# Two mixer stages in another order: attention worked between the heads' projections, the recurrence between the convolved columns and the output gates

## The reference

```
proj = h @ w_in          # columns: q 512, k 512, v 512 | qk 512, v 512, o 512, gates 8
# differential attention: 4 heads x 2 halves of 64, rotary q and k, mask by chunks of 64
a = softmax(q1 k1) - lam * softmax(q2 k2);  y_da = rmsnorm(a v) * (1 - lam_init)
# recurrence: 4 heads of 64 x 128
qk = silu(causal_conv(qk));  w = exp(D - m) * (q k);  y_ml = sigmoid(o) * rmsnorm((w v) / den)
y = concat(y_da, y_ml) @ w_out
```

## Time and profile before

| | |
|---|---|
| runs of the kernel | 2193.6, 2198.66, 2198.86 us (median 2198.66) |
| the profiled execution: time, span | 2192.0 us, 2190.2 us |
| PE, PEld, DVE, ACT, POOL busy | 91%, 66%, 38%, 29%, 2% of the span |
| mixer 0, from its gates to the next stage's first turned rows | 1331.90 to 1453.02 us |
| mixer 1, the same | 1864.90 to 1987.13 us |
| mean granted clock of the PE | 0.97 |

### The profile page before, as it was taken

One profiled execution on the slowest core, in us unless ns is written; L12 is line 12 of the kernel. 1 busy time (PEld: TensorE's weight loads), 2 busy tenths in 40 slices (PEclk: granted clock), 3 DMA queues, 4 the chain that ended last, 5 costly groups with the idle time before them and its releaser, 6 DMA issues.

```text
span 2190.2 us, 38271 instructions
## 1 busy us (share of the span) xinstructions
PE 1989.8 (91%) x17232; PEld 1452.0 (66%) x17232; DVE 827.9 (38%) x1259; ACT 627.5 (29%) x994; POOL 46.3 (2%) x99
## 2 busy tenths in 40 slices
PE   5998898888979898888979999789999999979998
PEld 3544344446764444444469988679988987957996
DVE  4111111115530111111165546655545555755552
ACT  2000000004520000000055445554435444555441
POOL 0000000000000000000000000010000000000000
PEclk8999999999999999999999999999999999989999
DMA  9899999995559999999955554236545554424552
GB/s 383 365 426 427 426 427 426 426 427 211 181 197 427 426 426 427 426 427 427 417 199 195 182 184 154 78 107 217 177 158 207 194 184 157 151 79 162 175 191 77
DMA packets 56768, 599.74 MB, mean 274 GB/s; under 512 B 6544, under 2 KB 6800, under 8 KB 9488
## 3 DMA queue, kind: packets, MB, share of 16 engines
q1 hardware_dynamic: 55440, 593.75, 68.4%
q10 hardware_dynamic: 1152, 3.41, 0.6%
HBM read 596.08 MB, written 1.05 MB: 273 GB/s over the span
## 4 chain that ended last, share of the span: by engine, by line
PE 66%; DMA 18%; DVE 6%; ACT 6%; issue 3%; POOL 1%; SPq 0%; DVEq 0%; POOLq 0%; ACTq 0%
PE PS L515 13%; PE PS L517 13%; PE PS L516 13%; PE PS L667 12%; DMA RING<-in_w_down 8%; PE PS L637 7%; DMA WK<-in_w_down 6%; DMA WK<-in_w_up 3%; PE PS L614 2%; PE PS L695 2%; ACT SPLIT L1300 1%; ACT JK L1294 1%; DMA RING<-in_units 1%; DVE SPLIT L1769 1%; POOL SM L474 1%
## 5 line engine op out<-in xcount | busy, mean ns | idle before, releaser
L1769 DVE TENSOR_TENSOR SPLIT<-RING,SPLIT 128x2048 fp32r<-128x2048 f32 (+2 forms) x178 | 400.9, 2258 | 265.7 <-ACT SPLIT L1300 265.5
L667 PE MATMUL PS<-RING,WK 128*32 128x512 f32 x816 | 367.8, 605 | 51.1 <-DMA RING<-in_w_down 29.4
L515 PE MATMUL PS<-HTH,SPLIT 128*128 128x256 f32 x1344 | 382.6, 285 | 0.0
L516 PE MATMUL PS<-HTL,SPLIT 128*128 128x256 f32 x1344 | 380.7, 283 | 0.0
L517 PE MATMUL PS<-HTH,SPLIT 128*128 128x256 f32 x1344 | 380.6, 283 | 0.0
L1300 ACT ACTIVATE SPLIT<-RING 128x2048 fp32r<-128x2048 f32 (+2 forms) x178 | 334.2, 1885 | 142.4 <-DMA RING<-in_units 132.3
L667 PEld LDWEIGHTS PS<-RING,WK 128*32 128x32 f32 x816 | 86.9, 111 | 294.5 <-issue 261.5
L515 PEld LDWEIGHTS PS<-HTH,SPLIT 128*128 128x128 f32 x1344 | 258.1, 192 | 0.5
L516 PEld LDWEIGHTS PS<-HTL,SPLIT 128*128 128x128 f32 x1344 | 258.1, 192 | 0.2
L517 PEld LDWEIGHTS PS<-HTH,SPLIT 128*128 128x128 f32 x1344 | 258.1, 192 | 0.0
L637 PE MATMUL PS<-RING,WK 128*32 128x128 f32 x7104 | 231.6, 274 | 10.6 <-issue 7.5
(11 more groups left out here) (331 smaller groups left out, 2019.7 us busy)
## 6 DMA issues: line engine op xcount, KB each, us to landing
RING<-in_units SPq DMA_DIRECT2D x171, 1024.0 KB, 4.9
RING<-in_w_gate SPq DMA_DIRECT2D x56, 2048.0 KB, 25.6
RING<-in_w_up SPq DMA_DIRECT2D x55, 2048.0 KB, 26.5
RING<-in_w_down SPq DMA_DIRECT2D x53, 2048.0 KB, 29.4
WK<-in_w_down SPq DMA_DIRECT2D x9, 2048.0 KB, 30.0
WK<-in_w_up SPq DMA_DIRECT2D x9, 2048.0 KB, 27.4
WK<-in_w_gate SPq DMA_DIRECT2D x8, 2048.0 KB, 24.8
RING<-in_w_down SPq DMA_DIRECT2D x3, 1024.0 KB, 21.7
```

What stands on the lines that cost most here:

```text
L515: pe.matmul(out, ll, rh, start=start, stop=False)
L516: pe.matmul(out, lh, rl, start=False, stop=False)
L667: t = pe.matmul(PS[32 * i:32 * i + 32, 4 + h, :], mo.HE[:, pb, 32 * f:32 * f + 32], v[:, c, 512 * h:512 * h + 512], start=f == 0, stop=f == 3)
L1769: dv.tensor_tensor(unit_part(u, 1), loaded(u), unit_part(u, 0).bitcast(F32), ALU.subtract).then_inc(s_lo, 1)
```

## The change

The lists of the mixer are rewritten; the number of matmuls, conversions and transfers stays. A head's q and k now lie side by side in one unit (u0+4 to u0+7), and the columns come after them (u0+8, u0+9). The heads use two PSUM banks instead of four, since banks 6 and 7 now serve the attention, so `head(i)` waits for the end of `rotate(i-2)` on DVE. The scores, probabilities and outputs of an attention head follow its projections; then come the columns; the output gates (`gate_rows`, once `last_rows`) stand between the steps of the recurrence, and the attention's results are turned there too. The recurrence's result is turned one row block at a time between the `out` steps, and all of block 1's `out` steps stand at the end. The exponentials of the recurrence move to a buffer of their own. POOL takes two short roots for the attention instead of a long one.

Of the lists of steps only the lines of after stand here (a "+" marks a line that was not there in the place before); the three lists are those of the PE, ACT and DVE, in this order. Line numbers of after are higher: `lo` is 1792, `hi` 1314, the DVE's part of `rotate` 2240 to 2245, of `scores` 2253 and 2257.

```diff
-HEAD_BANK = [5, 6, 7, 4]
-HEADS = [("q", 0), ("q", 1), ("k", 0), ("k", 1), ("q", 2), ("q", 3), ("k", 2), ("k", 3)]
-KEY_AT = [2, 3, 6, 7]
+HEAD_BANK = [5, 4]
...
-            def column(h):
-                u = u0 + 4 + h // 2
...
             def head(i):
-                u = u0 + 6 + i // 2
+                u = u0 + 4 + i // 2
                 hi, lo = unit_pair(u)
                 o = 128 * (i % 2)
                 pe.wait_ge(s_lo, u + 1)
-                pe.wait_ge(*((s_qkc, 4 * l + i + 1) if i < 4 else (s_qr, 4 + 8 * l + i - 3)))
+                if i == 1:
+                    pe.wait_ge(s_gv, 6 * l + 3)
+                elif i >= 2:
+                    pe.wait_ge(s_qr, 4 + 8 * l + i - 1)
                 for c in range(8):
-                    t = three(pe, pair(PS[:, HEAD_BANK[i % 4], 0:256]), (hi[:, c, o:o + 128], lo[:, c, o:o + 128]), both(c),
+                    t = three(pe, pair(PS[:, HEAD_BANK[i % 2], 0:256]), (hi[:, c, o:o + 128], lo[:, c, o:o + 128]), both(c),
                               c == 0, c == 7)
...
             def rotate(i):
                 pe.wait_ge(s_tq, 4 + 8 * l + i + 1)
-                pe.matmul(PS[:, HEAD_BANK[i % 4], 256:512], cs("swap"), mx.TQ[:, i % 2, :], start=True,
+                pe.matmul(PS[:, HEAD_BANK[i % 2], 256:512], cs("swap"), mx.TQ[:, i % 2, :], start=True,
                           stop=True).then_inc(s_sw, 1)
...
+            def column(i):
+                u = u0 + 8 + i // 2
...
+                if i == 0:
+                    pe.wait_ge(s_unc, 2 * l + 2)
+                    pe.wait_ge(s_dv, 2 * l + 2)
+                    pe.wait_ge(s_mvc, 2 * l + 2)
+                for c in range(8):
+                    t = three(pe, pair(PS[:, i, 0:256]), (hi[:, c, o:o + 128], lo[:, c, o:o + 128]), both(c), c == 0, c == 7)
+                t.then_inc(s_unit if i % 2 else s_mc, 1)
...
-                    pe.wait_ge(s_unc, 2 * l + 2)
                     pe.wait_ge(s_gv, 6 * l + 6)
+                    pe.wait_ge(s_qkc, 4 * l + 4)
...
                 else:
-                    pe.wait_ge(s_mvc, 2 * l + 1)
                     pe.wait_ge(s_cos, 4 * l + 4)
...
             def scores(h):
-                pe.wait_ge(s_qr, 4 + 8 * l + max(KEY_AT[h] + 1, 6))
+                pe.wait_ge(s_qr, 4 + 8 * l + 2 * h + 2)
                 for d in range(2):
                     if h:
                         pe.wait_ge(s_pm, 8 + 8 * l + 2 * (h - 1) + d + 1)
+                    if h >= 2:
+                        pe.wait_ge(*((s_yd0, 4 * l + h - 1) if d else (s_ptc, 8 + 4 * l + h - 1)))
...
             def weights(h):
                 pe.wait_ge(s_mw, 8 * l + 2 * h + 2)
-                if h:
-                    pe.wait_ge(s_ptc, 8 + 4 * l + h)
-                else:
-                    pe.wait_ge(s_qr, 4 + 8 * l + 7)
+                if h < 3:
+                    pe.wait_ge(s_pm, 8 + 8 * l + 2 * h + 3)
...
             def outs(h):
                 a = mx.AT[:, h % 2, :]
                 pe.wait_ge(s_ptc, 8 + 4 * l + h + 1)
-                if h == 0:
-                    pe.wait_ge(s_qr, 4 + 8 * l + 8)
-                else:
-                    pe.wait_ge(s_yd0, 4 * l + h)
+                if h < 3:
+                    pe.wait_ge(s_pm, 8 + 8 * l + 2 * h + 4)
...
+            def gate_rows(k, b):
+                u = u0 + 10 + k
                 hi, lo = unit_pair(u)
                 pe.wait_ge(s_lo, u + 1)
-                if u == u0 + 10:
-                    pe.wait_ge(s_ym, 4 * l + 3 + b)
+                if k == 0:
+                    pe.wait_ge(s_qr, 4 + 8 * l + 8)
...
-            def turn_heads(src, bank):
+            def turn_attention(z):
+                pe.wait_ge(s_ydn, 2 * l + z + 1)
...
+            def turn_recurrence(b):
+                pe.wait_ge(s_ymn, 8 * l + 4 * b + 4)
+                pe.wait_ge(s_ol, 8 + 12 * l + 2 * b + 2)
...
+                if k == 0:
+                    pe.wait_ge(*((s_ym, 4 * l + 4) if b else (s_mem, 4 * l + 4)))
                 for c in range(2):
-                    f = (4, 6, 0, 2)[k] + c
-                    pe.wait_ge(s_ol, 8 + 8 * l + (4 if k < 2 else 2 * k + c + 1))
+                    f = 2 * k + c
+                    pe.wait_ge(s_ol, 8 + 12 * l + f + 1 + (4 * b if f >= 4 else 0))
                     if c and before:
                         before()
...
             head(0)
             head(1)
             rotate(0)
             head(2)
             rotate(1)
+            to_tokens()
             head(3)
+            scores(0)
             rotate(2)
             head(4)
             rotate(3)
+            scores(1)
+            head(5)
+            weights(0)
+            rotate(4)
+            head(6)
+            outs(0)
+            rotate(5)
+            scores(2)
+            head(7)
+            weights(1)
+            rotate(6)
+            column(0)
+            outs(1)
+            rotate(7)
+            scores(3)
+            column(1)
+            weights(2)
+            column(2)
+            outs(2)
+            column(3)
+            weights(3)
+            gate_rows(0, 0)
+            outs(3)
+            decays(0)
+            gate_rows(0, 1)
             decays(1)
             sums(0)
+            turn_attention(0)
+            gate_rows(1, 0)
             decays(2)
             sums(1)
+            turn_attention(1)
             decays(3)
+            gate_rows(1, 1)
             sums(2)
             sums(3)
             out(0, 0)
             out(1, 0)
+            turn_recurrence(0)
             out(2, 0)
             out(3, 0, s_half)
+            turn_recurrence(1)
+            for k in range(4):
+                out(k, 1, s_unit, after if k == 3 else None)
...
+                    ac.wait_ge(*((s_unit, u0 + 5 + i // 2) if i % 2 else (s_mq, 4 * l + i // 2 + 1)))
                     if i >= 2:
                         ac.wait_ge(s_qr, 4 + 8 * l + i - 1)
-                    ac.activation(mx.TQ[:, i % 2, :], PS[:, HEAD_BANK[i % 4], 0:256], ACT.Copy).then_inc(s_tq, 1)
-                def column(h):
-                    ac.wait_ge(*((s_unit, u0 + 5 + h // 2) if h % 2 else (s_mc, 2 * l + h // 2 + 1)))
-                    ac.activation(mx.QK[:, h, 3:259], PS[:, HEAD_BANK[h], 0:256], ACT.Copy).then_inc(s_qkc, 1)
+                    ac.activation(mx.TQ[:, i % 2, :], PS[:, HEAD_BANK[i % 2], 0:256], ACT.Copy).then_inc(s_tq, 1)
...
+                def attention_turned(z):
+                    ac.wait_ge(s_yt, 4 * l + z + 1)
+                    ac.wait_ge(s_unit, u0 + 11)
...
+                head(0)
+                head(1)
                 ac.wait_ge(s_gv, 6 * l + 5)
                 ac.activation(mx.NEM[0:4, :], mx.NEM[0:4, :], ACT.Exp, scale=-1.0).then_inc(s_gx, 1)
                 hi(u0 + 8)
+                head(2)
                 hi(u0 + 9)
+                head(3)
+                scores(0)
+                head(4)
+                probs(0)
                 hi(u0 + 10)
                 head(5)
                 scores(1)
                 weights(0)
+                head(6)
                 probs(1)
+                outs(0)
+                head(7)
                 scores(2)
+                weights(1)
+                probs(2)
+                column(0)
+                outs(1)
+                hi(u0 + 11)
+                scores(3)
+                column(1)
+                weights(2)
+                column(2)
+                probs(3)
+                outs(2)
+                column(3)
+                weights(3)
+                outs(3)
+                ac.wait_ge(s_cov, 16 * l + 16)
+                for i in range(4):
+                    ac.activation(mx.CO[:, i, :], mx.CO[:, i, :], ACT.Silu).then_inc(s_cos, 1)
+                hi(u0 + 12)
+                decays(0)
+                hi(u0 + 13)
+                decays(1)
+                attention_turned(0)
+                sums(0)
+                decays(2)
+                attention_turned(1)
+                sums(1)
+                decays(3)
+                hi(u0 + 14)
+                sums(2)
+                sums(3)
                 ac.wait_ge(s_unit, u0 + 12)
                 for b in range(2):
+                    ac.activation(mx.SO[:, b, :], PS[:, 4 + b, :], ACT.Sigmoid).then_inc(s_so, 1)
                 hi(u0 + 15)
                 next_rows(SECOND[j + 1])
+                recurrence_turned(0)
+                recurrence_turned(1)
...
+                def attention_normed(z):
+                    yd = mx.YD.rearrange("p b (h n) -> p h b n", h=4)[:, 2 * z:2 * z + 2, :, :]
+                    rs = mx.RSD[:, 4 * z:4 * z + 4].rearrange("p (h b) -> p h b", h=2)
+                    dv.wait_ge(s_yrs, 2 * l + z + 1)
+                    for i in range(2):
...
+                rotate(0)
                 lo(u0 + 8)
+                rotate(1)
                 dv.wait_ge(s_gp, 2 * l + 2)
                 dv.tensor_copy(mx.UT, PS[:, 0, 0:8].rearrange("p (b h) -> p b h", b=2)).then_inc(s_unc, 1)
```

(34 more changed lines are left out.)

258 lines of the change are left out of this document (79 added, 179 removed).

## The result

The changed kernel takes 2211.32 us (median of 4 runs, 2210.36 to 2212.73) against 2196.13 us of the kernel before (4 runs, 2193.34 to 2198.86). The ratio is 1.007, with a 95% interval of 1.0052 to 1.0088, and the medians lie 15.2 us apart. The profiled execution took 2212.73 us with a span of 2210.9. That is 20.7 us more than the profiled one of before, since it is the longest of its four, while the one of before, at 2192.0 us, lies near the low end of that kernel's runs.

A forecast was written before the change was run, and what follows sets the result against it. The PE, 91% busy, bounds the kernel. New waits of 14.45 + 5.95 + 9.95 = 30.35 us a mixer against 17.6 + 1.0 give 11.75 more, taken as 10, so +20 for two mixers: 2215 us, range 2206 to 2224.

The forecast's parts named there:

- Heads: Attention heads and scores: the PE waits for DVE's rotations two heads back, 13.55 us a mixer, where nothing idled before.
- The floor with DVE at hand: Least wait for a rotation when DVE is free: 1.1 us at each of seven places, 7.4 us in all.
- Recurrence: Recurrence of each mixer: the PE waits for ACT's Silus and DVE's decays, 5.95 us in sum.
- The Silu's wait: Before `decays(0)`, which now needs all four Silus from ACT: the PE waits 3.3 us.
- the four small waits: In the recurrence: four more PE waits by the chain of exponential, product and mask, 1.0 us together.
- End: Mixer's end, from before `turn_recurrence(0)` to the next stage's entry: PE waits of 9.95 us in sum.
- The entry's wait: Next stage's entry, late because high and low parts go first: the PE waits 3.4 us instead of 0.9.
- The cut from 11.75 to 10 us: Added waits a mixer, taken as 10 since PE work, counted 2 us under the rows, fills part of them.
- bounds of 0 and 9 us: Limits a mixer for the PE's loss to a lower clock, forecast as before at 5 us.
- Waits at their floor: Rival: ACT and DVE come in time, waits 14.1 us a mixer against 18.6, kernel faster at 2186; chance 0.20.
- the clock falls among the heads: Rival: half of the eight heads run at clock 0.50, 6 us a mixer more, 2231 to 2235; chance 0.13.
- The extra 2.8 us a mixer: Two table-load switches on the new chain, by the skill page's 2.66 us a switch; would make the sum +25.

The follow-up runs named there:

- the first experiment: Changed kernel with the next stage's first two high and low parts moved ahead of `recurrence_turned(1)` on ACT and DVE; 2203.50 us, ratio 1.004.

## Why the prediction was right

The forecast was 2215 us and slower, for waits that add up to 30.35 us a mixer, with a mixer of 129 to 134 us. Measured were 2211.32 us, 26.0 us of waits in mixer 0 and 25.1 in mixer 1, and lengths of 130.8 and 131.7 us. The mechanism was as forecast, wait by wait. Point by point, in mixer 0:

- *Heads.* 13.55 us were forecast and 12.4 measured (8.8 on heads, 2.9 + 0.6 at `scores`), in eight waits at the named places (seven for DVE, one for ACT). Head by head: 1.81 for 1.85, 1.45 for 1.65, 2.98 for 2.75, 2.58 for 2.85, and 0.97 or 0.98 where 1.1 was taken three times. The floor with DVE at hand is thus a little under the forecast. Only the wait inside `scores(2)` was sized far off: 0.62 for 1.15 us. The experiments with four banks and with the rotations first show the cause. The last `weights` waited 0.87 us, for 0.9.
- *Recurrence.* The Silu's wait was 3.14 us, for 3.3. The 1.65 us before `decays(1)` did not show, and that is an error in size with a known cause: `gate_rows(0, 1)` ahead of it took 4.53 us instead of some 3, at a clock of 0.62, and this covered the wait. With the Silus first, where this group took 3.02 us, the wait stood there, with 2.06 us. Of the four small waits three showed, with 0.6 us, for 1.0.
- *End.* 2.82 us for 3.1 before `turn_recurrence(0)`, and 1.90 for 2.1 before `out(2, 0)`. The 1.35 us before `out(3, 0)` did not show: `out(2, 0)` began at the lower clock and ended later by about that much. The entry's wait was 4.26 us, for 3.4, the one wait of the end that came out larger. The cause is as forecast (high parts ahead of the squares), shown by the first experiment.
- *The sum.* Of 4.3 us of waits that did not come, 3.0 are the two hidden by matmuls at the lower clock. The forecast took +10 us a mixer, with the clock as before; the windows show +9.7 and +9.5, of which 7.4 are waits and 2.3 more time at the lower clock. So the total was nearer than its two parts, and that part is luck: the forecast's added waits were too many, and the clock's loss was larger than the 5 us by some 2. The cut from 11.75 to 10 us, for work that fills waits, rested on a count that no row shows; the rows show 11.75 - 4.4 = 7.4 us of added waits. The clock's loss lies inside its bounds of 0 and 9 us.
- *The rivals.* Waits at their floor did not come, since DVE's list put low parts and scores ahead of the rotations, as the argument against that rival said. Nor is its clock that stays up as long as no gap passes 3.3 us borne out: it fell behind waits of 2.98, 2.58 and 1.81 us here, and the earlier trace rows had it at 0.69 behind one of 1.3. That the clock falls among the heads came half true: two of eight heads ran at the lower clock in mixer 0 and three in mixer 1, not four. Four of mixer 0 did in the execution with the Silus first, whose heads have the same lists, so this rival was nearer than the profile of the changed kernel alone tells. On the gap the Trainium skill (TensorE: Matmul & The Clock Gate, section HAM oscillation) was right in that waits brought the clock down; here the waits of 2.98 and 2.58 us brought it down each time, that of 1.81 us in one mixer of two, and that of 1.45 us did not.
- *The table load.* The first Silu begins 1.29 us after the load's start, as in the earlier trace rows. The Sigmoid's load, the other switch, is the same: it starts at 1438.55 and the Sigmoid at 1439.84. The extra 2.8 us a mixer, by the figure of the Trainium skill (ScalarE: Activation LUTs, section What ACT_TABLE_LOAD costs), did not come.

What the prediction treated too lightly is how waits cover one another. It added them up, though a stretch at the lower clock or an earlier wait can hide the next: the Silu's wait, shortened by 2.8 us, gave back nothing in the time, and the entry's 4.3 us, with 0.9 us of clock on top, gave back 3.9.

What stays open is why the clock falls behind a wait in one mixer or execution and not in the next. The changed kernel's waits are 26.0 and 25.1 us in the two mixers of one execution, and its busy time is 104.8 and 106.5 us for the same matmuls. No forecast that goes by the lists alone can be sharper than that.

## What to carry to other kernels

When an order is written by hand for several engines, go through all the lists together, with a duration for each entry, and ask at each wait of the busiest engine what stands ahead of the entry that it waits for; an engine at 37% (DVE here) was late seven times among the eight heads of a stage. Buffers that are reused after two steps instead of four cost one round trip of the other engines (here about 1 us) at each use, and more wherever that engine's order puts something else first. Bulk work that nobody needs yet, such as conversions for a later stage, goes behind the short entry that somebody waits for, and into idle time.
